# The opening of a streaming-encoder layer: roots, low halves and a narrow first product for token tiles 0 and 1 alone

## The reference, cut to what matters

```
h    = x * rsqrt(mean(x^2) + eps) * g_pre_mix
P    = h @ w_in          -> [u_a | v_a | q | k | v_b]   (5120 columns)
...                      (spatial gating, stick-breaking attention, gates, merge, ConvFFN)
```

## Time and profile before

| | |
|---|---|
| median of three runs | 2177.4 us (2174.63 to 2178.53) |
| the profiled execution | 2178.22 us, span 2176.4 us |
| mean granted TensorE clock | 0.992 of full speed |
| PE busy over the span | 97% |
| DVE, ACT, POOL busy | 58%, 40%, 33% |

### The profile page before, as it was taken

One profiled execution on the slowest core, in us unless ns is written; L12 is line 12 of the kernel. 1 busy time (PEld: TensorE's weight loads), 2 busy tenths in 40 slices (PEclk: granted clock), 3 DMA queues, 4 the chain that ended last, 5 costly groups with the idle time before them and its releaser, 6 DMA issues. The chain is left out here.

```text
span 2176.4 us, 33742 instructions
## 1 busy us (share of the span) xinstructions
PE 2112.7 (97%) x13316; PEld 1997.6 (92%) x13316; DVE 1257.1 (58%) x1860; ACT 880.8 (40%) x1641; POOL 728.4 (33%) x454
## 2 busy tenths in 40 slices
PE   6999999999999999999999999999999999999997
PEld 5999999999899999998999988899999999888875
DVE  5036021000677888757656647588888888734565
ACT  4222211222777777755443122243433333323343
POOL 2325433453644544436565210003343333100000
PEclk9999999999999999999999999999999999999999
DMA  5115422655565555547665533211222222453654
GB/s 182 49 62 171 142 86 89 174 152 164 147 150 140 128 134 133 134 114 220 173 203 185 171 126 99 81 49 60 88 64 88 67 83 75 180 199 125 215 193 145
DMA packets 305651, 285.15 MB, mean 131 GB/s; under 512 B 51078, under 2 KB 270422, under 8 KB 305494
## 3 DMA queue, kind: packets, MB, share of 16 engines
q1 hardware_dynamic: 292432, 252.88, 39.7%
q10 hardware_dynamic: 10822, 21.99, 2.7%
q0 software_dynamic: 2240, 8.13, 1.0%
HBM read 203.59 MB, written 79.35 MB: 130 GB/s over the span
## 5 line engine op out<-in xcount | busy, mean ns | idle before, releaser
L294 PE MATMUL p_psB<-hT_lo,w_hi 128*128 128x364 f32 x888 | 295.7, 333 | 2.4 <-issue 2.4
L294 PE MATMUL p_psB<-hT_hi,w_lo 128*128 128x364 f32 x888 | 293.2, 330 | 0.0
L294 PE MATMUL p_psB<-hT_hi,w_hi 128*128 128x364 f32 x888 | 292.5, 329 | 0.0
L1185 DVE TENSOR_TENSOR_SCAN p_rest<-p_rest 128x896 f32<-128x896 f32 (+7 forms) x128 | 213.3, 1676 | 85.7 <-ACT p_rest L1108 85.6
L958 POOL TENSOR_TENSOR p_weights<-p_weights,p_rest 128x895 f32<-128x895 f32 (+7 forms) x128 | 161.0, 1263 | 208.1 <-DVE p_rest L1185 208.1
L582 ACT ACTIVATE p_line<-p_psB 128x364 f32<-128x364 f32 x108 | 51.2, 474 | 373.0 <-PE p_psB L294 373.0
L2721 DVE TENSOR_TENSOR p_w_lo<-p_w_raw,p_w_hi 128x512 fp32r<-128x512 f32 (+1 forms) x168 | 160.8, 962 | 54.3 <-ACT p_w_hi L2517 54.2
L294 PEld LDWEIGHTS p_psB<-hT_lo,w_hi 128*128 128x128 f32 x888 | 168.1, 189 | 3.4 <-issue 2.8
L294 PEld LDWEIGHTS p_psB<-hT_hi,w_hi 128*128 128x128 f32 x888 | 168.1, 189 | 0.0
L294 PEld LDWEIGHTS p_psB<-hT_hi,w_lo 128*128 128x128 f32 x888 | 167.7, 189 | 0.0
L2517 ACT ACTIVATE p_w_hi<-p_w_raw 128x512 fp32r<-128x512 f32 (+1 forms) x186 | 139.1, 772 | 64.7 <-DVE p_rows L2740 34.4
(11 more groups left out here) (388 smaller groups left out, 6086.4 us busy)
## 6 DMA issues: line engine op xcount, KB each, us to landing
p_w_raw<-in_w_down SPq DMA_DIRECT2D x66, 512.0 KB, 3.9
p_w_raw<-in_w_up SPq DMA_DIRECT2D x44, 512.0 KB, 5.0
w_raw<-in_w_in SPq DMA_DIRECT2D x40, 512.0 KB, 3.9
hid_scratch<-p_rows ACTq DMA_DIRECT2D x22, 545.0 KB, 2.8
p_kT<-k_hi_scratch SPq DMA_DIRECT2D x32, 256.0 KB, 4.4
p_kT<-k_lo_scratch SPq DMA_DIRECT2D x32, 256.0 KB, 5.0
w_raw<-in_w_gate SPq DMA_DIRECT2D x16, 512.0 KB, 4.6
p_raw_v<-in_cache_sb_v SPq DMA_DIRECT2D x8, 1024.0 KB, 6.2
```

Source lines behind the costliest of these rows:

```text
L294: last = nc.tensor.matmul(out[:, 0:CH], stat[:, slot, w], mov[:, k, c], start=(at == 0), stop=(at == 3 * KT - 1))
L1185: nc.vector.tensor_tensor_scan(src, src, src, 1.0, ALU.mult, ALU.bypass).then_inc(s("scanned"), 1)
```

## The change

DVE computes the roots of tiles 0 and 1 by themselves and scales those two tiles, then computes the root of tile 2 alone, then makes the low halves of tiles 0 and 1, and only then scales tile 2. ACT squares four tiles before it rounds off tiles 0 and 1, and one more before tile 2. PE turns tiles 0 and 1, runs half of product 0 on the 258 columns that those two tiles fill, turns tile 2, runs the other half, and then runs all of product 0 again for the last 106 columns of the chunk. Product 0 so has 48 matmuls in place of 24. Tiles 5 and 8 are turned after products 2 and 5, and no longer after products 1 and 4. SP asks for weight block 1 after token tile 3 (before: after tile 5) and for block 2 after tile 5 (before: after all nine).

```
                     if m == 2:
                         sp.dma_start(g_row[:, :], ...)
+                    if m == 3:
+                        load(1)
                     if m == 5:
-                        load(1)
-                load(2)
+                        load(2)
...
+                def first_part(cols, ks):
+                    for k in ks:
+                        w = slice(k * P, (k + 1) * P)
+                        last = three_passes(nc, psB[:, 0, cols], ring.hi[:, 0, w], ring.lo[:, 0, w], hT[0][:, k, cols], hT[1][:, k, cols],
+                                            k == 0, k == KT - 1)
+                    return last
+
-                for m in range(3):
+                for m in range(2):
                     turn_h(m)
+                ring.ready(pe, 0)
+                pe.wait_ge(s("hT_hi"), 2)
+                pe.wait_ge(s("hT_lo"), 2)
+                first_part(slice(0, col(2)), range(0, 4))
+                turn_h(2)
+                first_part(slice(0, col(2)), range(4, KT))
+                pe.wait_ge(s("hT_hi"), 3)
+                pe.wait_ge(s("hT_lo"), 3)
+                first_part(slice(col(2), CH), range(KT)).then_inc(s("group"), 1)
                 for q, (n, c) in enumerate(ORDER):
-                    if q in (0, 3, 6):
+                    if q == 0:
+                        continue
+                    if q in (3, 6):
                         pe.wait_ge(s("hT_hi"), q + 3)
                         pe.wait_ge(s("hT_lo"), q + 3)
...
                     if q in (1, 4):
-                        for m in range(q + 2, q + 5):
-                            turn_h(m)
+                        turn_h(q + 2)
+                        turn_h(q + 3)
+                    if q in (2, 5):
+                        turn_h(q + 3)
...
-                for m in range(6):
+                for m in range(4):
                     square(m)
-                for m in range(3):
+                for m in range(2):
                     h_hi(m)
-                for m in range(6, TILES):
+                square(4)
+                h_hi(2)
+                for m in range(5, TILES):
                     square(m)
...
+                dve.wait_ge(s("table"), 1)
+                roots(0, 2)
+                dve.wait_ge(s("g_ready"), 16)
+                norm(0)
+                norm(1)
+                roots(2, 3)
+                h_lo(0)
+                h_lo(1)
+                norm(2)
+                h_lo(2)
+                for m0 in (3, 6):
+                    roots(m0, m0 + 3)
                     for m in range(m0, m0 + 3):
-                        ...
+                        norm(m)
                     for m in range(m0, m0 + 3):
                         h_lo(m)
```

More of the change, by code:

```diff
@@ L667, in h_lo, with roots, norm @@
                                             ALU.subtract).then_inc(s("hT_lo"), 1)
[L669 to L673, removed]
-                    rsqrt_steps(nc, ch, ss[:, g], rstd[:, g], tmp[:, g], 1.0 / D)
-                    if m0 == 0:
-                        dve.wait_ge(s("g_ready"), 16)
+                def roots(m0, m1):
+                    g = slice(m0, m1)
+                    dve.wait_ge(s("squares"), m1)
+                    rsqrt_steps(nc, ch, ss[:, g], rstd[:, g], tmp[:, g], 1.0 / D)
+                def norm(m):
+                    r = rows(m)
+                    nc.vector.scalar_tensor_tensor(out=x_tok[0:r, m, :], in0=x_tok[0:r, m, :], scalar=rstd[0:r, m:m + 1],
+                                                   in1=g_row[0:r, :], op0=ALU.mult, op1=ALU.mult).then_inc(s("h_ready"), 1)
+                dve.wait_ge(s("table"), 1)
[10 more added lines that the diff above has]
+                    roots(m0, m0 + 3)
                     for m in range(m0, m0 + 3):
-                        r = rows(m)
-                        nc.vector.scalar_tensor_tensor(out=x_tok[0:r, m, :], in0=x_tok[0:r, m, :], scalar=rstd[0:r, m:m + 1],
-                                                       in1=g_row[0:r, :], op0=ALU.mult, op1=ALU.mult).then_inc(s("h_ready"), 1)
+                        norm(m)
                     for m in range(m0, m0 + 3):
```

## The result

| | before | changed |
|---|---|---|
| median | 2177.36 us (20 runs, 2173.88 to 2180.99) | 2185.44 us (20 runs, 2178.53 to 2190.33, and one far outside, 5537.35) |
| the profiled execution | 2178.22 us, span 2176.4 | 2190.33 us, span 2188.5 |
| mean granted TensorE clock, mean over runs | 0.9925 (34 runs) | 0.9906 (19 runs) |

The far one is left out of the ratio, the means and the clock. The forecast was 2180.5 with a range of 2175 to 2186, so the time lies near the upper end, past the main case and past the slower rival (2183.7).

The account below looks back on a forecast made before the run. PE, busy for 97% of the span, was taken as the bound; +2.3, +1.0 and -0.2 us summed to +3.1 on the profiled 2178.2, giving 2181.3, and 2180.5 after taking off 0.8 for that execution; range 2175 to 2186.

Parts of the forecast that it names:

- main case: Opening: one block's split holds tile 2's root chain, product 1 starts at 31.5, time 2180.5 us; chance 0.43.
- slower rival: Opening: splits of blocks 1 and 2 both hold tile 2's root chain, which ends at 23; 2183.7 us; chance 0.25.
- First turn: PE's turn of tile 0 starts at 13.2 in place of 14.93, a gain of 1.7 us.
- Splits: POOL's split of block 1 moves from 17.4 to 14.3; block 2 lands at 18.8 to 19.8.
- By that rule the three one-input steps could wait as well.: DVE's one-input steps of tile 2's chain might also wait for POOL's split, ending the chain 0.6 us later.
- The chain of tile 2: DVE's root steps start at 14.35 during block 1's split and end at 19.4, undisturbed at 16.75.
- both splits: Blocks 1 and 2 are both split during tile 2's chain, which ends at 23; 2183.7 us; chance 0.25.
- The earlier request gains nothing: Weight blocks were not late before, so asking sooner wins no time and only moves POOL's split of block 1.
- Product 0: Matmuls 0.22 us apart at 258 columns, 0.11 at 106; product 1 starts at 31.5 for 29.23, +2.3 us.
- Tiles 5 and 8: Turned one product later: stalls of 2.4 and 1.45 us replace two of 1.6; +1.0 and -0.2 us.
- The slow stretch: Half-clock stretch at 54.17 to 57.58, costing 1.3 us: one kept, so zero change, bounds -1.3 and +1.3.

Follow-up runs that it names:

- changed again: The changed kernel, unaltered, measured a second time: mean 2184.5 us, ratio 1.0028 to the kernel before.
- turns back: The changed kernel with tiles 5 and 8 turned after products 1 and 4 again: mean 2181.4 us, ratio 1.0022 to the kernel before.
- whole product: The changed kernel with product 0 in one piece behind all three turns: mean 2185.4 us, ratio 1.0036 to the kernel before.
- splits held: The changed kernel, but POOL leaves weight block 1 unsplit until DVE has scaled tile 2: mean 2180.2 us, ratio 1.001 to the kernel before.
- requests back: The changed kernel with the weight blocks requested where the kernel before requests them: mean 2180.8 us, ratio 1.0019 to the kernel before.
- both back: The changed kernel with both the weight-block requests and the turns of tiles 5 and 8 in their old places: mean 2177.9 us, ratio 1.0002.
- turns only: The kernel before with only tiles 5 and 8 turned one product later: mean 2179.8 us, ratio 1.0013.
- lows first: The changed kernel with the low halves of tiles 0 and 1 made ahead of tile 2's root chain: mean 2185.2 us, ratio 1.0035.
- Parts only: The kernel before with product 0 as 24 matmuls of 258 columns and 24 of 106, behind all three turns: mean 2175.0 us, ratio 0.9984.
- filled: The kernel before with product 0 in two column parts behind all three turns, and tiles 5 and 8 turned inside products 2 and 5: mean 2172.4 us, ratio 0.9975.
- Turns inside: The kernel before with tiles 5 and 8 turned within products 2 and 5, behind nine of their 24 matmuls: mean 2175.3 us, ratio 0.9988.
- requests only: The kernel before with only the sooner weight-block requests: mean 2180.1 us, ratio 1.0016.

## Why the prediction came out low

**First turn, "This part gains 1.7 us".** Too much. The first turn came at 13.72 for 13.2: the chain began at 9.05, and its first step, with two elements per partition, stood 1.03 us beside block 0's split, which the sum had left out. Over the profiles the first turn starts at 13.42 to 14.00 with the roots of two tiles apart (eight profiles) and at 14.07 to 14.93 with three in one chain (six): 0.9 us in the mean. It cost the sum nothing, since the later chain set the start of product 0.

**Splits.** Right: block 1's split at 14.15 for 14.3, block 2's at 18.52 and 19.61 for 18.8 to 19.8. In the rows of the kernel before, the chain of tiles 3 to 5 has a third long step that the prediction does not name (27.69 to 28.69, beside POOL's masking of another tensor, to 28.67). Its 5.5 us include that step, and no term rests on it.

**"By that rule the three one-input steps could wait as well."** The Trainium skill (SBUF — State Buffer, "Who interferes with whom") was weighed there. Two-input steps obeyed it in every profile, in both directions: POOL's L152 took 1.52 us beside a scaling. The one-input steps of tile 2's chain did not wait, 0.15 us each beside a split; those with two or three elements per partition did (below).

**The chain of tile 2, "I take 19.4".** The mechanism held, the size was off. It ended at 20.4 to 20.7 in three profiles (changed again, turns back, whole product: block 2's high half caught the last step) and at 22.2 in one. Product 1 so started at 32.5 to 34.4, not 31.5. From 32.50 on the main case's own terms hold: its sum puts product 6 at 62.4, and it stood at 63.34 in changed again, 0.94 later, all of it from the chain. The chance of 0.25 for both splits was of the right order: one profile of four.

**"The earlier request gains nothing."** Right; with them back 4.0 us are won, and splits held shows why.

**Product 0.** Right: 0.214 us between 258-column matmuls at the slow pace (0.22 forecast), 0.112 between those of 106 (0.11), 2.53 us from the turn of tile 2 to the 106 columns (2.42), 1.1 us of it uncovered, as its own numbers imply.

**Tiles 5 and 8.** Right: stalls of 2.42 and 1.46, +0.7 us from product 1 to product 6 (+0.8).

**"The slow stretch ... so zero, with -1.3 and +1.3 as bounds."** This is the term that was too small. The first 60 us were the only ones it looked at. Over whole executions 8.7 us more ran at the half clock (standard error 1.7), 2.5 to 3.3 us of time, past the bound of 1.3. Summed anew: +4.0 of waits (product 6 of changed again, with one slow stretch ahead of it in either kernel) and +2.5 to +3.3 of clock is 6.5 to 7.3, for 7.4 measured.

**The range.** That it holds the time is in part luck. Its upper end was set by the case in which both splits fall on the chain, one profile of four; the main case with its chain put right gives about 4 us, and the rest of the way was mostly clock, of which its bounds held 1.3 us at most.

What tips the clock is not settled. In all fourteen profiles the half-clock stretches behind the opening stand at the same few places of the kernel (near 540, 1000, 1280, 1400, 1470 and 1890 to 1905 us, and the last 7 to 9 us); which of them occur, and how long they last, differs. In the first 75 us they came to between 0 and 10.2 us (3.4 before, 0 and 6.8 in the two profiles of the changed kernel). Late turns raised its share in three pairs (turns back to changed 33.8 to 41.2, both back to requests back 31.9 to 36.9, before to turns only 32.5 to 38.8), and they bring a stall of 2.4 us in place of one of 1.6. But sooner requests alone raised it as much (38.8), with only a wait of 2.77 us for 0.83 in the opening, and lows first raised it most. Parts only and filled, the two kernels in which PE has no wait above 1.6 us behind its first turn, have the lowest share (29.3). Turns inside, which has no stall of 1.6 us but still waits 2.42 ahead of product 0, has no lower share than the kernel before (35.2 for 33.2). That is a correlation; why a change in the first 60 us shows in stretches at 540 or 1906 us no run tells.

## What to carry to other kernels

An earlier request is not free when its data is not needed: ask what its landing starts on another engine, and which dependent chain that will hold. A producer that is moved to directly ahead of its user loses the work that covered its delay; put it inside that work, with enough matmuls on either side, and the wait is gone altogether. Where PE is the bound, compare the granted clock over many runs as well as the waits: here a third or more of the loss was clock, and one profile shows only a few of its stretches.

## What the runs showed that was not expected

- **Small steps on DVE.** TENSOR_SCALAR on one element per partition passed beside a POOL split in every profile in which it met one (0.15 us). On two or three elements it stood to the split's end: 1.03 us at 9.05 in the changed kernel, 2.35 us at 25.66 in requests back.
- **Narrow matmuls.** At the full clock matmuls of 106 columns start 0.112 us apart, those of 258 columns 0.12 and those of 364 0.166: between 106 and 258 columns the width is almost free, and the second pass for 106 columns costs nearly what the first did.
- **POOL waits as well.** Its L152 took 1.91 us and its L155 3.20 us beside DVE's scalings in requests only, for 1.04 and 2.35 alone: in these rows whichever of the two started first held the other.
